# The per-token rate of the scan's group normalisation: one power on GpSimd in place of a root on ScalarE and four reciprocals on VectorE

## The reference

```python
y = ys[0] + jnp.flip(ys[1], axis=1)
mu = jnp.mean(y, axis=-1, keepdims=True)
var = jnp.mean(jnp.square(y - mu), axis=-1, keepdims=True)
y = (y - mu) * lax.rsqrt(var + GN_EPS) * heads(gn_w.astype(f32)) + heads(gn_b.astype(f32))
bonus = jnp.sum(rh * heads(kf) * r_k, axis=-1, keepdims=True) * vh
out = ((y + bonus).reshape(B_, L, D_A) * gate).astype(h.dtype)
```

## Time and profile before

| | us |
|---|---|
| median of 3 runs | 2405.17 (2402.86 to 2405.58) |
| the profiled execution | 2401.35 |
| its span | 2399.4 |
| TensorE busy | 2243.7 (94%) |
| VectorE busy | 936.9 (39%) |
| ScalarE busy | 397.0 (17%) |
| GpSimd busy | 167.3 (7%) |

### The profile page before, as it was taken

How to read it: one execution, slowest core, us unless ns; L and a number is a source line. 1 busy time by engine, 2 the same in 40 slices (tenths; PEclk the granted TensorE clock), 3 DMA queues, 4 the chain that set the end, 5 groups by cost and what they waited for, 6 DMA issues and landing times. The chain is left out here.

```text
span 2399.4 us, 56100 instructions
## 1 busy us (share of the span) xinstructions
PE 2243.7 (94%) x23412; PEld 1282.6 (53%) x23412; DVE 936.9 (39%) x1965; ACT 397.0 (17%) x685; POOL 167.3 (7%) x162
## 2 busy tenths in 40 slices
PE   5998989999888889999999999889998999999997
PEld 2446777777676765544444444545555444444444
DVE  2357666676757621211111111479613111111113
ACT  2022323232323201000000000211312000000001
POOL 1001010100101000000000000000000000000000
PEclk8998999999999999999999999899999999999999
DMA  9981010101000035799999999502036999999995
GB/s 369 386 316 32 2 33 2 32 2 32 13 22 21 2 122 197 268 383 393 395 396 393 394 396 390 193 1 70 1 140 255 395 397 394 393 397 393 392 392 172
DMA packets 181670, 538.56 MB, mean 224 GB/s; under 512 B 12545, under 2 KB 54145, under 8 KB 181410
## 3 DMA queue, kind: packets, MB, share of 16 engines
q1 hardware_dynamic: 175202, 515.16, 55.8%
q0 software_dynamic: 6336, 21.63, 3.8%
HBM read 510.81 MB, written 25.95 MB: 224 GB/s over the span
## 5 line engine op out<-in xcount | busy, mean ns | idle before, releaser
L2108 PE MATMUL ps<-raw,xs 128*64 128x512 f32 x3072 | 673.8, 596 | 4.0 <-PEq L2102 3.9
L2108 PEld LDWEIGHTS ps<-raw,xs 128*64 128x64 f32 x3072 | 217.7, 137 | 431.0 <-issue 429.6
L2120 PE MATMUL ps<-raw,xs 128*32 128x256 f32 x6144 | 342.3, 380 | 3.2 <-PEq L2102 3.2
L2120 PEld LDWEIGHTS ps<-raw,xs 128*32 128x32 f32 x6144 | 195.1, 110 | 134.0 <-issue 10.4
L2299 DVE SCALAR_TENSOR_TENSOR h<-h,ps 128x768 f32<-128x768 f32 x32 | 30.5, 954 | 461.9 <-DVEq L2298 461.9
L1644 DVE COPY_PREDICATED wk<-m,ps 128x128 f32<-128x128 uint8 x360 | 101.4, 352 | 116.4 <-DVEq L1640 116.2
L2426 PE MATMUL ps<-h,raw 128*128 128x512 f32 (+1 forms) x448 | 124.7, 440 | 7.2 <-PEq L2417 7.2
L2227 ACT ACTIVATE h<-ps 128x768 f32<-128x768 f32 x32 | 25.9, 811 | 595.1 <-ACTq L2226 595.1
L900 PE MATMUL ps<-h,wk 128*128 128x512 f32 (+1 forms) x416 | 121.4, 438 | 1.5 <-PEq L1216 1.3
L1030 PE MATMUL ps<-wk 64*64 64x64 f32 x2400 | 102.9, 223 | 14.5 <-PEq L1006 13.8
L1044 PE MATMUL ps<-wk 64*64 64x64 f32 x2400 | 98.5, 219 | 5.0 <-PEq L1006 3.2
(11 more groups left out here) (333 smaller groups left out, 2643.9 us busy)
## 6 DMA issues: line engine op xcount, KB each, us to landing
raw<-in_moe_w_gate SPq DMA_DIRECT2D x64, 2048.0 KB, 18.0
raw<-in_moe_w_up SPq DMA_DIRECT2D x64, 2048.0 KB, 20.0
raw<-in_moe_w_down SPq DMA_DIRECT2D x64, 2048.0 KB, 19.1
wk<-in_mod_w SPq DMA_DIRECT2D x24, 2048.0 KB, 12.1
wk<-in_ev_w_in SPq DMA_DIRECT2D x18, 512.0 KB, 5.3
raw<-in_od_w_in SPq DMA_DIRECT2D x4, 2048.0 KB, 15.2
hrow<-rows SPq DMA_DIRECT2D x10, 512.0 KB, 2.9
ysum<-low SPq DMA_DIRECT2D x10, 512.0 KB
```

What stands on the lines that cost most here:

```text
L2108: last = pe.matmul(ps[to:to + CAPS, bank_of(kind, ee)], XS[ee][:, c, 0:CAPS], raw[:, slot(l, 2 * m + c // 4), c % 4, 8 * to:8 * to + 512], ...
L2120: last = pe.matmul(ps[to:to + 32, bank_of(kind, ee) + 1, 0:256], XS[ee][:, c, CAPS:], raw[:, slot(l, 2 * m + c // 4), c % 4, 8 * to:8 * to ...
```

## The change

The variance is still scaled and gets its epsilon on ScalarE, now by Identity in place of the root, for the tail inside the six inverses. GpSimd then raises it to the power −1/2, as one tensor-tensor instruction of 128x640 against a broadcast constant. This stands behind the joining add in GpSimd's program. VectorE's pieces 0 to 3 go from the levels; it waits for the power ahead of `y_scaled`, which stands behind level 2 as before; `y_shifted` moves from level 2 to level 3, in front of `y_gated`. The last pair's own tail, after its last scan step, keeps root and four reciprocals.

```diff
+            half_power = ca(1)
...
-            TAIL = ((0, 1), (2, 3), (4, 5), (6,), (7,), ())
+            TAIL = ((), (), (4,), (5, 6), (7,), ())
...
-                    def y_root():
+                    def y_root(pooled):
 
                         act.wait_ge(sem("yvar_ready"), 1).then_inc(sem("yvar_ready"), -1)
-                        act.activation(root, pair(1), ACT.Sqrt, scale=1.0 / HD, bias=eps[:, 2:3]).then_inc(act_done, 1)
-                        done("yroot_ready")
+                        if pooled:
+                            act.activation(root, pair(1), ACT.Identity, scale=1.0 / HD, bias=eps[:, 2:3]).then_inc(act_done, 1)
+                            done("yvar_scaled")
+                        else:
+                            act.activation(root, pair(1), ACT.Sqrt, scale=1.0 / HD, bias=eps[:, 2:3]).then_inc(act_done, 1)
+                            done("yroot_ready")
...
-                        y_root()
+                        y_root(True)
...
-                            y_root()
+                            y_root(False)
...
+                    pool.memset(half_power, -0.5).then_inc(pool_done, 1)
+                    pool.wait_ge(pool_done, 3).then_inc(pool_done, -3)
...
                         pool.tensor_tensor(mat[:, :, 0, :, 3], mat[:, :, 0, :, 3], mat[:, :, 1, :, 3], ALU.add).then_inc(pool_done, 1)
                         pool.wait_ge(pool_done, 1).then_inc(pool_done, -1)
                         pool.sem_inc(sem("mat_joined"), 1)
+                        pool.wait_ge(sem("yvar_scaled"), 1).then_inc(sem("yvar_scaled"), -1)
+                        pool.tensor_tensor(root, root, half_power.broadcast_to([P, T]), ALU.pow).then_inc(pool_done, 1)
+                        pool.wait_ge(pool_done, 1).then_inc(pool_done, -1)
+                        pool.sem_inc(sem("yrate_ready"), 1)
...
-                        if n < 4:
-                            y_rate(n)
-                        elif n == 4:
+                        if n == 4:
+                            dve.wait_ge(sem("yrate_ready"), 1).then_inc(sem("yrate_ready"), -1)
                             y_scaled()
```

More of the change, by code:

```diff
@@ L1420, in _ @@
                     pool.memset(gnv, 0.0).then_inc(pool_done, 1)
-                    pool.wait_ge(pool_done, 2).then_inc(pool_done, -2)
+                    pool.memset(half_power, -0.5).then_inc(pool_done, 1)
+                    pool.wait_ge(pool_done, 3).then_inc(pool_done, -3)
                     pool.sem_inc(sem("s0_zero"), 1)
```

## The result

The changed kernel takes **2900.58 us** (2897.8 to 2904.86, four runs) against 2405.38 (2402.86 to 2407.37): a ratio of 1.2061, interval 1.204 to 1.2082. The profiled execution takes 2899.34 us, its span is 2897.4. It was forecast at 2398.8; it became 495 us slower.

A forecast was written before the change was run, and what follows sets the result against it. TensorE, busy 94% of the span, bounds the kernel, so only its idle spells count; 4.5 + 1.6 + 0.3 = 6.4 us saved, power covered at 0, gives 2398.8 us from 2405.17; 8-in-10 range 2394.5 to 2425.

The forecast's parts named there:

- The power's length: GpSimd's 128x640 power per pair: 13.8 us taken, 27.5 us upper end; up to 20.8 us (last pair 17.2) costs nothing.
- The rule that I set aside: Skill page's 4 cycles per element per dependent fp32 step; with 25 guessed steps the power takes 53 us, total near 2597 us.
- The cover: From the power's start to VectorE's scaling after level 2: 19.3 us plus 1.5 free; last pair 17.2 us.
- rival 1: Power outlasts its cover, VectorE and TensorE wait before level 3: at 27.5 us 44 us lost, 2442 us; chance 0.20.
- Rival 2: Gap at level 1 refilled by ScalarE's copy, the projection or VectorE's first copies: about 2402 us; chance 0.18.
- The 0.90 us per ordinary pair: TensorE's 1.10 us spell before level 1's `correct(2)` shrinks to 0.20 without reciprocals: 4.5 us over five pairs.
- The last pair: Its inverse, without projections between levels, gets shorter steps from the new tail table: 1.6 us saved, bounds 0.8 and 2.5.
- The table load in pair 0: ScalarE's 1.28 us load before `decay_tanh(0)` goes, ahead of a copy TensorE awaits: 0.3 us saved, bounds 0 and 1.28.
- Rival 3: Power locks VectorE out, delaying level 0's first copies 13 us in each of six inverses: 2477 us; chance 0.05.
- The moved tail: Shift, bonus and gate between levels 3 and 4 of ordinary pairs: costs nothing, at most 1.8 us per pair if uncovered.

The follow-up runs named there:

- Runs 2 to 6: Changed kernel with power on 160, 96, 128 columns (exponent 1), then one partition; kernel before plus a scratch power: 2437.81, 2399.96, 2402.43, 2897.77, 2403.14 us.
- run 4: Changed kernel with GpSimd's power on 128 of 640 columns against a full tile of ones (exponent 1): 2402.43 us, one execution.
- multiply run: Changed kernel with GpSimd's power replaced by a multiply of the same operands: 2401.91 us against 2404.02 for the kernel before, ratio 0.9994; executed twice.
- 8: Changed kernel with a multiply for the power, repeated word for word to compare TensorE's idle spells: six inverses 237.7 us, against 242.2 in the kernel before.
- run 6: Kernel before plus, in each pair, an unused GpSimd power of 160 columns on a scratch tile: 2403.14 us against 2404.1, ratio 0.9993.
- run 2: Changed kernel with GpSimd's power on 160 of 640 columns, the rest keeping the variance: 2437.81 us, ratio 1.0149.

## Why the prediction was wrong, point by point

- **The power's length: the step that failed.** "Two such functions, 13.8 us, is what I take; four, 27.5 us, is my upper end." It is 102.35 us, 82 times the multiply of the same shape. The scale came from VectorE, whose reciprocal costs 5.5 multiplies. It says nothing about what GpSimd does for a power, and no row of GpSimd in the trace held anything but adds, multiplies, copies, fills and DMA issues. The upper end was no bound at all but another guess. The forecast should have left the decisive cost open over a wide factor: 13.8 us lay only 7 us under the 20.8 at which the move turns, so 0.28 was too small a chance for slower.
- **The rule that I set aside.** The estimate worked out from the Trainium skill (GPSIMD Engine Reference, Performance pitfalls for Q7 kernels), a serial chain of 4 cycles for each of 25 steps, the steps being my guess, was 53 us: half of the 102.35 measured, where mine was a seventh. I gave it no chance, though it was the only statement at hand on what such work costs there. Runs 2 to 6 show that the price does not hang on the values tried or on the number of partitions, which fits a fixed serial sequence per column; they don't show the sequence itself.
- **The cover and the arithmetic of rival 1 held.** Forecast 19.3 us (17.2 in the last pair) plus 1.5 free. Measured from the power's start to the end of level 2's last copies: 19.4 in pair 2, 17.2 in the last pair, 19.2 to 22.0 in the others, the longer ones where TensorE spells fall in. The 1.5 us were free indeed (run 4). With the true price its formula gives 5 × (102.35 − 20.8) + (102.35 − 17.2) = 492.9 us; the six inverses take 496.3 us more than the multiply's. Mechanism and place were right, its price was short by 75 us per pair and its chance of 0.20 far too low.
- **Rival 2** was right in part. The gap was partly refilled, but by none of the waits that it named: by 1.3 to 1.7 us of spells without a semaphore (8).
- **The 0.90 us per ordinary pair** was right where a pair is undisturbed (6.79 to 5.87). One pair was read for five, and such spells as pairs 1 and 4 showed before were not looked for.
- **The last pair:** 35.46 to 34.89 and 33.96 us in the two multiply runs, 0.6 and 1.5 us against 1.6 forecast.
- **The table load in pair 0:** 0.3 us forecast. TensorE's wait of 1.33 us is 1.05 in the multiply run: 0.28, in one execution of each.
- **Rival 3,** the lock, was right to have little: run 6.
- **The moved tail** cost nothing in ordinary pairs: the step of level 3 to 4 is 7.22 before and 7.22 to 7.24 in the multiply runs.
- **Half clock after each wait:** not forecast, since no long wait was. It made level 3 some 1.5 us longer per pair (run 2), which about cancels what was free: in the changed kernel the six steps from level 2 to 3 are 494.8 us longer than the multiply's, for waits of 496.9.

## What to carry to other kernels

Before work moves to an engine, look for a row in which that engine does that very operation; without one, its price is unknown by more than a factor scaled from another engine can hold, and the chance must say so. Then compute the cover, as here, and read off at what price the move turns: if that point lies inside the unknown, measure the operation on a narrow slice first. A small gain that comes from taking work off a gap may be had by moving the work into idle time ahead of it, on the same engine.

## What the runs showed of the hardware

- A tensor-tensor power on GpSimd took 0.33 us + 0.1594 us per fp32 column, for widths of 96 to 640 on 128 partitions, for exponents −1/2 and 1, and as long on 1 partition as on 128 (640 columns); a multiply of 128x640 took 1.25 us.
- A power of 25.8 us on GpSimd ran beside VectorE's instructions with one and with two operands in SBUF and lengthened none of them.
- TensorE's granted clock was 0.50 over most of a wait of 81 us and until 5 us after work resumed, and 1.00 behind that. It also was 0.50 behind TensorE waits of 2.7 to 8.3 us in one run (five of five), not behind one of 1.8 us there nor behind one of 3.1 us in another.
- TensorE showed idle spells without a semaphore in two recurring places, of 0.60 to 1.15 and 1.10 to 1.79 us, and in others that changed from one execution of a program to the next.
